# A streamed weight kernel on one core: within each half unit, all products of the high weights first, the products of the low weights last

## The chip, the cores and the metric

The kernel runs on one core of a Trainium2 chip. The metric is the device time in microseconds of one execution; lower is better. The engines are TensorE (PE, with its weight loads shown as PEld), VectorE (DVE), ScalarE (ACT), GpSimd (POOL) and SyncE (SP), which issues the stream's DMAs.

## The reference, cut to what matters

Two transformer-like blocks on 256 tokens of width 1024, all in float32. The first block mixes tokens in three ways, then has a gated feed-forward part; the second has a convolution, sparse attention, a memory attention and a layer of 16384 experts, of which each token takes a few. Nearly all of the time goes to matrix products with weights that are read once from memory:

```python
z = rmsnorm(h, norm_mix_g[l]) @ w_in[l]
...
h = h + jnp.concatenate([o_a, o_b, o_c], axis=-1) @ w_out[l]
...
u = hn @ w_up
...
return (jax.nn.silu(gate) * val) @ w_down
...
h = h + peer(rmsnorm_2(h, peer_norm_g[l]), peer_w_q[l], peer_sub_keys[l], peer_u[l], peer_v[l])
```

## The kernel before

All weights lie in one stream of units of 128 x 1024 numbers (512 KB), four units to a chunk. SP reads them in turn into four buffers `raw` (line 386). Float32 precision is had from three products of a faster type: each number is split into a high part and a low part, and the product is high x high + low x high + high x low.

A unit is split in two halves of 512 columns. `split_hi` (line 425, ScalarE) makes `w_hi` of a half and increments `s_hi1` (first half) or `s_hi` (second). `split_lo` (line 432, VectorE, or GpSimd in the woven streams and beside the selection) waits for that, makes `w_lo = raw - w_hi` and increments `s_lo1` or `s_lo`. There are two buffers each of `w_hi` and `w_lo`, so the split of a unit waits until TensorE has used the unit two before: the last product of a half increments `s_use1` or `s_use`. `halves_of_unit` (line 435) lists, for both halves, the semaphore of the low part and the one of use.

TensorE (`product3`, line 495; line 500 in the profile) takes, for each tile, the three products one behind another. Each is a weight load of 128 x 128 (PEld) and a matmul (PE). Two layouts occur. In a feature unit the weights are the loaded operand and x of 256 tokens is streamed: a half has four tiles k, 12 products of 256 columns (ps_chunk<-x_hi,w_hi in the profile). In a token unit x is loaded and 512 columns of weights are streamed: a half has one tile k and two groups t of 128 tokens, 6 products of 512 columns (ps_chunk<-w_hi,x_hi, or ps_misc<-w_hi,hid_hi). Ahead of a half TensorE waits for its low part, which comes after the high part.

The streams, in order: the mixers of the first block (to 276 us), in which `woven_products` (line 610) gives out each half in two pieces (some = 0 and 1), placed by an order written out by hand (MIXERS_ORDER, MIXERS_2_ORDER, MEMORY_ORDER) among small products of other strands; ffn_up by `multiply` (line 519), beside which VectorE does eight taps of a convolution per chunk (line 1808) between its splits; ple_proj and ffn_down by `rows_of` (line 1864); ple_gate by `multiply`; the second block's mixers and the memory, woven again; peer_q by `multiply`; 36 early rows of the experts by `u_products` (line 2704) while VectorE picks the experts (line 2603 and on): of them 32 stand ahead of some transposes (line 2687) that need VectorE's picks, and ScalarE computes in each row a gelu (line 2723), sends it off and splits a later unit; then 32 more rows between small products of the gates (line 2829); 68 units of v by `v_unit` (line 2890); and 60 pairs of a u row and a v row. In the first chunk behind a new x (`first_two`, `woven_first_two`, `woven_first_halves`, and token chunks with `by_k` or `x_made`) the products follow the making of x.

Of the kernel before, what the change touches and what calls it, by code (L numbers as in the profile page):

```python
# [215 lines left out]
def build(nc, stream, cols, rows, consts0, consts1, consts2, x, mem, positions, small_w, cmp_w1, cmp_w2, peer_keys, p_t, out):  # L216
    ctx = ExitStack()
    with ctx:
# [216 lines left out]
        halves_of_unit = ((0, s_lo1, s_use1), (1, s_lo, s_use))  # L435

# [58 lines left out]
        def product3(e, o, stationary, moving, start, stop, low_x=None):  # L495
# [6 lines left out]
            return last  # L502

# [21 lines left out]
        def multiply(name, token_major, by_k=(), between=None):  # L525
# [37 lines left out]
            def body(e, slot, n, half):  # L563
                room(e, n)
                fresh = isinstance(n, int) and n == first and by_k
                for q in range(UNITS):
# [8 lines left out]
                    for part, made, used_up in halves_of_unit:  # L575
                        e.wait_ge(made, n * UNITS + (q + 1))
                        if token_major:
                            k = 2 * q + part
                            if fresh:
                                e.wait_ge(*by_k[k][0])  # L580
                            for t in range(TT):
# [3 lines left out]
                                                by_k[k][1] if fresh else None)  # L585
# [24 lines left out]
        def woven_products(u, n, q, part, some, token_major, ps, left, x_made=None, tile_end=False):  # L610
# [3 lines left out]
            _, made, used_up = halves_of_unit[part]  # L614

            def run(e):
                e.wait_ge(made, u + 1)
                if token_major:
                    if q == 0 and part == 0 and n:
                        e.wait_ge(*left[some])  # L620
                    k = 2 * q + part
                    if x_made:
                        e.wait_ge(*x_made[k][0])
                    last = product3(e, ps[:, some * CW:some * CW + width],
                                    [x[:, k, some * P:(some + 1) * P] for x in (x_hi, x_lo)],
                                    [a[:, part * CW:part * CW + width] for a in w], k == 0, k == KD - 1,
                                    x_made[k][1] if x_made else None)
                else:
                    if q % 2 == 0 and part == 0 and some == 0 and n:
                        e.wait_ge(*left[q // 2])  # L630
# [8 lines left out]
            pe.quiet(run)  # L639

        def woven_first_two(u, ps, left, by_k, i):

# [2577 lines left out]
```

## Time and profile before

| | us |
|---|---|
| Median of 3 runs | 1593.06 |
| Lowest and highest run | 1588.82, 1595.22 |
| Span of the profiled execution | 1586.8 |
| TensorE matmuls busy | 1526.8 (96%) |
| VectorE busy | 1168.7 (74%) |
| ScalarE busy | 851.7 (54%) |
| GpSimd busy | 353.0 (22%) |

The span runs from the first to the last instruction of one profiled execution; the time of a run also holds what lies around it. Times in the rows below are microseconds from the span's start unless marked ns. Matmuls are pipelined: a matmul's own duration (0.28 us for 256 columns, 0.39 for 512) is longer than the distance between the starts of two of them, and it is that distance that tells the pace.

### The profile page before, as it was taken

What the parts mean: (1) busy time and instruction counts of PE and PEld (TensorE: products, weight loads), DVE (VectorE), ACT (ScalarE), POOL (GpSimd) and SP (SyncE); (2) the same over time, 40 slices, a digit from 0 to 9 for tenths busy, and PEclk for the clock granted to TensorE, in tenths of its full rate; (3) what the DMA queues carried; (4) which work ended last, traced back from release to release, by engine and by line L of the source; (5) the groups of instructions that cost most, each with busy time, mean ns of one, the idle gap of its engine ahead of it and who ended that gap; (6) DMA issues with size and microseconds to landing.
All of it is one profiled execution on the core that took longest, in us unless ns stands there. A gap on an engine that the chain in (4) does not pass through costs nothing.

```text
span 1586.8 us, 32061 instructions
## 1 busy us (share of the span) xinstructions
PE 1526.8 (96%) x10720; PEld 1374.3 (87%) x10720; DVE 1168.7 (74%) x2312; ACT 851.7 (54%) x1573; POOL 353.0 (22%) x265
## 2 busy tenths in 40 slices
PE   9899998999999899899999999999999999999997
PEld 7789987999887785698998999988888899999996
DVE  4788676788747577454499678889999777777776
ACT  5664445655548654565455455554444554454445
POOL 3333322011000331222067865640000000000000
PEclk9999999999999999999999999999999999999999
DMA  8332345555565720354656655467777656656564
GB/s 293 113 120 94 94 146 161 167 170 175 183 186 175 244 68 1 91 176 151 193 153 198 200 173 151 158 191 243 244 236 245 202 189 188 187 186 185 185 187 157
DMA packets 89289, 272.22 MB, mean 172 GB/s; under 512 B 9984, under 2 KB 27520, under 8 KB 88832
## 3 DMA queue, kind: packets, MB, share of 16 engines
q1 hardware_dynamic: 65520, 238.06, 47.9%
q10 hardware_dynamic: 23696, 33.17, 6.6%
q8 instruction: 48, 0.79, 0.2%
q14 instruction: 25, 0.20, 0.0%
HBM read 259.13 MB, written 12.06 MB: 171 GB/s over the span
## 4 chain that ended last, share of the span: by engine, by line
PE 77%; DVE 13%; ACT 4%; issue 2%; DMA 1%; POOL 1%; ACTq 0%; DVEq 0%; SPq 0%; POOLq 0%
PE ps_chunk L500 43%; PE ps_misc L500 22%; PE ps_misc L300 5%; PE ps_misc L2829 3%; PE ps_chunk L300 2%; DVE ffn_arena L1808 1%; DVE w_lo L432 1%; ACT w_hi L425 1%; POOL w_lo L432 1%; DVE mixers_arena L2607 1%; DVE mixers_arena L2608 1%; DVE mixers_arena L2604 1%; PE ps_chunk L507 1%; PE ps_misc L945 1%; DMA raw<-in_stream 1%
## 5 line engine op out<-in xcount | busy, mean ns | idle before, releaser
L425 ACT ACTIVATE w_hi<-raw 128x512 fp32r<-128x512 f32 (+2 forms) x898 | 547.0, 627 | 489.0 <-PE ps_chunk L500 280.8
L432 DVE TENSOR_TENSOR w_lo<-raw,w_hi 128x512 fp32r<-128x512 f32 x663 | 485.6, 748 | 256.4 <-ACT w_hi L425 246.4
L500 PE MATMUL ps_chunk<-x_hi,w_hi 128*128 128x256 f32 x1792 | 518.1, 289 | 15.3 <-POOL w_lo L432 7.6
L500 PE MATMUL ps_chunk<-x_hi,w_lo 128*128 128x256 f32 x1792 | 507.2, 283 | 0.0
L500 PE MATMUL ps_chunk<-x_lo,w_hi 128*128 128x256 f32 x1792 | 506.9, 283 | 0.0
L432 POOL TENSOR_TENSOR w_lo<-raw,w_hi 128x512 fp32r<-128x512 f32 (+2 forms) x237 | 310.1, 1323 | 517.6 <-ACT w_hi L425 453.3
L500 PEld LDWEIGHTS ps_chunk<-x_hi,w_hi 128*128 128x128 f32 x1792 | 343.2, 192 | 27.3 <-POOL w_lo L432 12.3
L500 PEld LDWEIGHTS ps_chunk<-x_hi,w_lo 128*128 128x128 f32 x1792 | 343.7, 192 | 2.7 <-issue 0.2
L500 PEld LDWEIGHTS ps_chunk<-x_lo,w_hi 128*128 128x128 f32 x1792 | 343.4, 192 | 0.0
L500 PE MATMUL ps_misc<-w_hi,hid_hi 128*128 128x512 f32 x516 | 201.7, 391 | 1.6 <-DVE hid_lo L2933 1.6
L500 PE MATMUL ps_misc<-w_hi,hid_lo 128*128 128x512 f32 x516 | 201.5, 390 | 0.0
L500 PE MATMUL ps_misc<-w_lo,hid_hi 128*128 128x512 f32 x516 | 200.7, 389 | 0.0
L300 PE MATMUL ps_misc<-mixers_arena 128*128 128x128 f32 (+9 forms) x820 | 111.0, 304 | 8.2 <-ACT mixers_arena L975 3.5
L500 PEld LDWEIGHTS ps_misc<-w_hi,hid_hi 128*128 128x128 f32 x516 | 97.1, 188 | 20.6 <-issue 1.7
L500 PEld LDWEIGHTS ps_misc<-w_lo,hid_hi 128*128 128x128 f32 x516 | 96.9, 188 | 20.7
L300 PEld LDWEIGHTS ps_misc<-mixers_arena 128*128 128x128 f32 (+3 forms) x820 | 94.7, 188 | 22.1 <-issue 8.5
L500 PEld LDWEIGHTS ps_misc<-w_hi,hid_lo 128*128 128x128 f32 x516 | 97.1, 188 | 17.7
L500 PE MATMUL ps_chunk<-w_hi,x_hi 128*128 128x512 f32 (+2 forms) x256 | 101.8, 398 | 7.2 <-POOL w_lo L432 4.6
L500 PE MATMUL ps_chunk<-w_hi,x_lo 128*128 128x512 f32 (+2 forms) x256 | 97.8, 382 | 0.0
L500 PE MATMUL ps_chunk<-w_lo,x_hi 128*128 128x512 f32 (+2 forms) x256 | 97.8, 382 | 0.0
L2929 DVE TENSOR_TENSOR xn<-row,peer_arena 128x256 f32<-128x256 f32 x128 | 80.7, 631 | 8.8 <-PE ps_misc L500 6.7
L2812 DVE TENSOR_TENSOR xn<-xn,ps_chunk 128x1024 bf16<-128x1024 bf16 x64 | 43.8, 684 | 33.0 <-PE ps_misc L2829 24.2
(411 smaller groups left out, 1667.9 us busy)
## 6 DMA issues: line engine op xcount, KB each, us to landing
raw<-in_stream SPq DMA_DIRECT2D x452, 512.0 KB, 3.6
early_rows<-row ACTq DMA_DIRECT2D x68, 128.0 KB, 1.7
row<-early_rows ACTq DMA_DIRECT2D x66, 128.0 KB, 3.3
memory_kv<-mixers_arena ACTq DMA_DIRECT2D x4, 512.0 KB, 5.0
mixers_arena<-in_cmp_w ACTq DMA_DIRECT2D x1, 2048.0 KB, 9.3
mixers_arena<-memory_kv ACTq DMA_DIRECT2D x4, 512.0 KB, 6.9
mixers_arena<-in_consts ACTq DMA_DIRECT2D x1, 1729.0 KB, 9.8
row<-in_rows ACTq DMA_DIRECT2D x3, 512.0 KB, 7.2
```

The lines of the kernel that those rows point to most:

```text
L300: return lambda e: e.matmul(out, lhsT, rhs, start=start, stop=stop, skip_group_check=True)
L425: e.activation(w_hi[q % 2][:, s], raw[q][:, s], ACT.Copy).then_inc(made, 1)
L432: e.tensor_tensor(w_lo[q % 2][:, s], raw[q][:, s], w_hi[q % 2][:, s].bitcast(F32), ALU.subtract).then_inc(made, 1)
L500: last = e.matmul(o, stationary[a], moving[b], start=start and i == 0, stop=stop and i == 2, skip_group_check=True)
L507: e.matmul(o, a[:, k * P:(k + 1) * P], x_hi[:, k, :], start=start and i == 0, stop=False, skip_group_check=True)
L945: done = pe.do(lambda e, i=i, s=s: e.transpose(ps[0:rows_out, i * P:(i + 1) * P], s, ident), *needs, *free)
L1808: e.scalar_tensor_tensor(out=o, in0=ps_chunk[slot][:, piece * T:(piece + 1) * T - lag], scalar=col[:, bass.ds(at + (2 - lag), 1)], in1=o, ...
L2604: lambda e, i: e.match_replace(out=rest[:, i, :], in_to_replace=values[:, i, 0:8], in_values=src[:, i, :], imm_value=-3e38),
L2607: lambda e, i: e.max_index(iu[:, i, 0:8], values[:, i, 0:8], src[:, i, :]),
L2812: e.tensor_tensor(twos(hot[g % 2]), iota_16.rearrange("p (n two) -> p n two", two=2).unsqueeze(1).broadcast_to(wide(2)), of_group(places_b ...
L2829: last = e.matmul(ps_misc[:, g % 2, i * P:(i + 1) * P], hot[g % 2][:, i, 1, :], gated_hot[g % 2][:, i, piece, :], start=piece == 0, stop=p ...
L2929: e.tensor_tensor(own[b], gel[slot], g, ALU.mult).then_inc(s_own, 1)
```

## The change

A list `high_of_half` names the semaphore of the high part of each half. In each half unit TensorE now waits for the high part alone, takes all products of the high weights (with x high and x low), waits for the low part, and takes the products of the low weights last. In the woven streams the two pieces of a half are cut anew: a feature half gives the high products of three tiles, then those of the fourth, the wait and the four low products; a token half gives three of its four high products, then the fourth, the wait and two low products. Left as before are the first two units behind a new x, token chunks whose x is being made, the last unit of a token stream, and in the woven projections chunk 0 and the last unit.

```diff
+        high_of_half = (s_hi1, s_hi)
...
+        def high_weights(e, o, w, k):
+
+            for x in (x_hi, x_lo):
+                e.matmul(o, w[0][:, k * P:(k + 1) * P], x[:, k, :], start=k == 0 and x is x_hi, stop=False,
+                         skip_group_check=True)
+
+        def low_weights(e, o, w, tiles):
+
+            for k in tiles:
+                last = e.matmul(o, w[1][:, k * P:(k + 1) * P], x_hi[:, k, :], start=False, stop=k == KD - 1,
+                                skip_group_check=True)
+            return last
...
                         else:
-                            for k in range(4 * part, 4 * part + 4):
-                                last = product3(e, ps_chunk[slot][:, q * T:(q + 1) * T],
-                                                [a[:, k * P:(k + 1) * P] for a in w],
-                                                [x[:, k, :] for x in (x_hi, x_lo)], k == 0, k == KD - 1)
+                            o = ps_chunk[slot][:, q * T:(q + 1) * T]
+                            tiles = range(4 * part, 4 * part + 4)
+                            e.wait_ge(high_made, n * UNITS + (q + 1))
+                            for k in tiles:
+                                high_weights(e, o, w, k)
+                            e.wait_ge(made, n * UNITS + (q + 1))
+                            last = low_weights(e, o, w, tiles)
                         last.then_inc(used_up, 1)
...
+            def by_weights(e):
+
+                k = 2 * q + part
+                outs = [ps[:, t * CW:t * CW + width] for t in range(TT)]
+                hi, lo = (a[:, part * CW:part * CW + width] for a in w)
+                if some == 0:
+                    e.wait_ge(high_made, u + 1)
+                    for t in range(TT):
+                        if q == 0 and part == 0 and n:
+                            e.wait_ge(*left[t])
+                        high_tokens(e, outs[t], k, t, hi, x_hi)
+                        if t == 0:
+                            high_tokens(e, outs[t], k, t, hi, x_lo)
+                    return
+                high_tokens(e, outs[1], k, 1, hi, x_lo)
+                e.wait_ge(made, u + 1)
+                for t in range(TT):
+                    last = low_tokens(e, outs[t], k, t, lo)
+                last.then_inc(used_up, 1)
...
         def u_products(e, b, w, u, tiles, part):
 
             _, made, used_up = halves_of_unit[part]
+            o, weights = ps_chunk[b][:, 0:T], (w_hi[w], w_lo[w])
+            e.wait_ge(high_of_half[part], u + 1)
+            for k in tiles:
+                high_weights(e, o, weights, k)
             e.wait_ge(made, u + 1)
-            for k in tiles:
-                last = product3(e, ps_chunk[b][:, 0:T], [a[w][:, k * P:(k + 1) * P] for a in (w_hi, w_lo)],
-                                [x[:, k, :] for x in (x_hi, x_lo)], k == 0, k == KD - 1)
-            if k % 4 == 3:
-                last.then_inc(used_up, 1)
+            low_weights(e, o, weights, tiles).then_inc(used_up, 1)
```

`rows_of` and `v_unit` are changed in the same way as token halves.

## Rows read from the trace of the kernel before

**Rows 1.** The page: the span; busy time by engine; chain that ended last, by engine.
```profile
span 1586.8 us, 32061 instructions
...
PE 1526.8 (96%) x10720; PEld 1374.3 (87%) x10720; DVE 1168.7 (74%) x2312; ACT 851.7 (54%) x1573; POOL 353.0 (22%) x265
...
PE 77%; DVE 13%; ACT 4%; issue 2%; DMA 1%; POOL 1%; ACTq 0%; DVEq 0%; SPq 0%; POOLq 0%
```

**Rows 2.** Waits, whole span: who <- whom: us in total, times, longest.
```profile
PEld ps_chunk L500 <- POOL w_lo L432: 18.3, 27, 2.9
...
PEld ps_chunk L500 <- DVE w_lo L432: 9.7, 15, 2.0
```

**Rows 3.** Chain that ended last in order of time: start, length, what.
```profile
750.71 40.57 PE ps_chunk L500 x336
...
1054.54 185.23 PE ps_misc L500 x816
```

**Rows 4.** Timeline of TensorE in ffn_up: start, length, instruction [idle before].
```profile
391.96 0.28 PE L500 MATMUL ps_chunk<-x_lo,w_hi 128*128 128x256 f32 x1
392.52 0.39 PE L500 MATMUL ps_chunk<-x_hi,w_hi 128*128 128x256 f32 x1 [0.28 <-DVE w_lo L432]
392.74 0.28 PE L500 MATMUL ps_chunk<-x_hi,w_lo 128*128 128x256 f32 x1
```

**Rows 5.** Waits of the weight loads, 0 to 60 us.
```profile
PEld ps_chunk L500 <- POOL w_lo L432: 1.2, 2, 0.9
```

**Rows 6.** Waits of the weight loads, 60 to 100 us; chain, 11 to 95 us.
```profile
PEld ps_chunk L500 <- DVE w_lo L432: 3.4, 2, 2.0
...
85.38 2.05 PE ps_chunk L300 x16
```

**Rows 7.** 276 to 420 us: waits; timeline of VectorE; busy time (instructions) of a chunk.
```profile
PEld ps_chunk L500 <- DVE w_lo L432: 5.5, 11, 1.1
...
391.77 2.50 DVE L432 TENSOR_TENSOR w_lo<-raw,w_hi 128x512 fp32r<-128x512 f32 x4 [0.22 <-DVE ffn_arena L1808]
...
380.47:392.52 12.05, 11.77 (x97) 11.57 (x97) 10.22 (x19) 7.19 (x14) 1.56 (x1) 1.00 0.54 174
```

**Rows 8.** 480 to 530 us: waits; timeline of ScalarE and TensorE.
```profile
PEld ps_chunk L500 <- POOL w_lo L432: 5.7, 4, 2.9
...
527.48 1.15 ACT L425 ACTIVATE w_hi<-raw 128x512 fp32r<-128x512 f32 x2 [3.03 <-DMA raw<-in_stream]
...
529.51 0.80 PE L500 MATMUL ps_chunk<-w_hi,x_hi 128*128 128x512 f32 x1 [2.68 <-POOL w_lo L432]
```

**Rows 9.** Waits of the weight loads, 660 to 800 us.
```profile
PEld ps_chunk L500 <- POOL w_lo L432: 1.0, 1, 1.0
```

**Rows 10.** The selection, 799 to 904 us: waits, then timelines of the engines.
```profile
PEld ps_chunk L500 <- POOL w_lo L432: 8.5, 18, 1.8
...
799.57 0.36 PE L500 MATMUL ps_chunk<-x_hi,w_hi 128*128 128x256 f32 x1
...
831.02 0.39 ACT L2723 ACTIVATE row<-ps_chunk 128x256 f32<-128x256 f32 x1 [1.00 <-PE ps_chunk L500]
...
832.74 2.72 POOL L432 TENSOR_TENSOR w_lo<-raw,w_hi 128x512 fp32r<-128x512 f32 x2 [0.62 <-ACT w_hi L425]
...
864.32 1.28 ACT L2635 ACT_TABLE_LOAD   x1 [0.73 <-ACT row L2723]
...
891.82 0.43 DVE L2680 CAST mixers_arena<-mixers_arena 128x512 bf16<-128x512 f32 x1
...
893.71 1.41 DVE L2680 CAST mixers_arena<-mixers_arena 128x512 bf16<-128x512 f32 x1
...
902.66 0.60 PE L2687 MATMUL ps_chunk<-ident_iota,mixers_arena 128*128 128x128 f32 x4
```

**Rows 11.** Timeline of the last row's products; chain at ple_gate's first chunk.
```profile
1576.43 0.62 PE L2907 MATMUL ps_misc<-w_lo,hid_hi 128*128 128x512 f32 x2
1576.88 0.62 PE L2907 MATMUL ps_misc<-w_hi,hid_hi 128*128 128x512 f32 x2
...
480.67 20.70 PE ps_chunk L500 x90
```

More of the change, by code:

```diff
@@ new lines, in by_tiles @@
+            def by_tiles(e):
+                o = ps[:, q * T:(q + 1) * T]
+                tiles = range(4 * part, 4 * part + 4)
+                if some == 0:
+                    e.wait_ge(high_made, u + 1)
+                    if q % 2 == 0 and part == 0 and n:
+                        e.wait_ge(*left[q // 2])
+                    for k in tiles[:3]:
+                        high_weights(e, o, w, k)
+                    return
+                high_weights(e, o, w, tiles[3])
+                e.wait_ge(made, u + 1)
+                low_weights(e, o, w, tiles).then_inc(used_up, 1)
@@ L616, in run @@
             def run(e):
                 e.wait_ge(made, u + 1)
[L618 to L630, printed above, removed]
-                    for k in range(4 * part + 2 * some, 4 * part + 2 * some + 2):
-                        last = product3(e, ps[:, q * T:(q + 1) * T],
-                                        [a[:, k * P:(k + 1) * P] for a in w],
-                                        [x[:, k, :] for x in (x_hi, x_lo)], k == 0, k == KD - 1)
+                if q == 0 and part == 0 and n:
+                    e.wait_ge(*left[some])
@@ L635, in run @@
+                k = 2 * q + part
+                if x_made:
+                    e.wait_ge(*x_made[k][0])
+                last = product3(e, ps[:, some * CW:some * CW + width],
+                                [x[:, k, some * P:(some + 1) * P] for x in (x_hi, x_lo)],
+                                [a[:, part * CW:part * CW + width] for a in w], k == 0, k == KD - 1,
+                                x_made[k][1] if x_made else None)
                 if some:
@@ L638, in run @@
                     last.then_inc(s_tile, 1)
-            pe.quiet(run)
+            pe.quiet(by_tiles if not token_major else run if x_made or by_token else by_weights)
         def woven_first_two(u, ps, left, by_k, i):
@@ L1112, in woven_projection @@
                     woven_products(u, n, q, part, some, True, ps_chunk[n % 2], ((s_ev, n - 1),) * 2,
-                                   tile_end=last and part == 1)
+                                   tile_end=last and part == 1, by_token=chunk == 0 or last)
                     if (part, some) == (0, 0):
@@ L1864, in rows_of, with times @@
             def rows_of(e, u, x, k, out, begin, end):
+                def times(t, half, x, w, start, stop):
+                    return e.matmul(out(t, half), x[:, k, t * P:(t + 1) * P], w[u % 2][:, half * CW:(half + 1) * CW],
+                                    start=start, stop=stop, skip_group_check=True)
                 for half, made, used_up in halves_of_unit:
+                    e.wait_ge(high_of_half[half], UNITS * first + u + 1)
+                    for t in range(TT):
+                        times(t, half, x[0], w_hi, begin, False)
+                        times(t, half, x[1], w_hi, False, False)
                     e.wait_ge(made, UNITS * first + u + 1)
                     for t in range(TT):
-                        last = product3(e, out(t, half), [a[:, k, t * P:(t + 1) * P] for a in x],
-                                        [w[u % 2][:, half * CW:(half + 1) * CW] for w in (w_hi, w_lo)], begin, end)
+                        last = times(t, half, x[0], w_lo, False, end)
                     last.then_inc(used_up, 1)
```

41 lines of the change are left out of this document (31 added, 10 removed).

## The prediction

> **What bounds the kernel now.** I read the page first: in the profiled execution (span 1586.8 us) TensorE is busy 96% of the time and 77% of the chain that ended last [rows 1]. So only two things can move the time: the pace of one product, and the gaps between products.
>
> The pace: in a steady stream 336 products of 256 columns take 40.57 us (121 ns each; 120 ns from start to start inside it), and 816 products of 512 columns take 185.23 us, 227.0 ns each [rows 3]. The second stretch crosses 136 half units, each with its wait for the low half, and shows no cost for them. A whole feature unit is 24 x 0.12 = 2.88 us, the eight high products of a half are 0.96 us, the four of a token half are 0.91 us.
>
> The gaps: the view of waits says that the weight loads of line 500 stood 18.3 us for a low half made by GpSimd (POOL) and 9.7 us for one made by VectorE, in 42 places [rows 2]. That is all the change can take, except that a stall also spoils the start: in the timeline the product after it starts 220 ns before the next, not 120 (392.52 to 392.74) [rows 4]. So a stall removed gives back its length and 0.10 us. At 391.96 TensorE was due again at 392.08 and began at 392.52, the low half being done at 392.46; its high half had long been made.
>
> **The change, part by part.** Removed: no product, no load, no split. Each half unit has the same products in another order and releases its buffer at its last one, as before. So no split and no DMA (SP's queue) is issued later; where TensorE comes earlier they move earlier. Added: one wait in each half unit that is changed, some 840 of about 900 (448 + 258 + 128 + 44 halves, from the counts of high products 1792/4, 516/2, 256/2, 88/2 on the page, less the first two units and the by-token ones that stay).
>
> Behind the low wait on TensorE stand the low products and everything of the other strands; before, the same stood behind it from the start of the half. VectorE is given 0.91 to 0.96 us longer in plain streams, and 0.7 us and the work of other strands between in the woven ones. The cover of the new wait is the 0.96 us of queued products; without it a wait costs the 0.10 us of a new start.
>
> The terms, by stage:
>
> 1. Start. Two waits of together 1.2 us for GpSimd's low half [rows 5]. In both the high half had been made by the time TensorE came (it must have been over 1 us earlier, since GpSimd takes 1.3 us for a low half [rows 10]). Both go: 1.2 + 2 x 0.10, less 0.1 where the high half is just made, 1.3 us. The chain runs through both on its way to VectorE. Bounds 0 and 1.4.
>
> 2. Mixers, 60 to 100 us. Two waits for VectorE's low half, 3.4 us [rows 6], and one for GpSimd's of the like, of which 0.96 us each could go. I count nothing: the chain there is VectorE's own, and TensorE's next step of it, at 85.38, waited for VectorE again [rows 6]. What is late next is the same VectorE. Bounds 0 and 2.9.
>
> 3. ffn_up and the begin of ffn_down: 11 waits, 5.5 us [rows 7], about one in each chunk of 12.05 us. In each VectorE does the eight older taps and then the low half of unit 2: 391.77 to 392.46 [rows 7], while TensorE is due at 392.08 and would need it at 392.08 + 0.96 = 393.04. So 0.58 us of slack is left, and VectorE is busy 10.22 of 12.05 us and has to fit 11.5 [rows 7]: it does. 5.5 + 11 x 0.10 = 6.6; the first of them keeps 0.3, since its high half is late too: 6.3 us. Bounds 4 and 6.6.
>
> 4. Second block, 480 to 530 us: four waits, 5.7 us [rows 8]. One lies in a chunk whose x is being made (that code is unchanged). Two lie ahead of a DMA that lands at 527.5 whatever TensorE does. At the last ScalarE waits 3.03 us for that DMA, the high half is made by 528.11, TensorE starts at 529.51 [rows 8]: 528.17 instead, 1.35 us. Bounds 0.5 and 2.8 (a part of what lies ahead of the DMA may come through too).
>
> 5. Memory, at 683: one wait of 1.0 us [rows 9], with its start 1.1; I take 1.05. Bounds 0 and 1.1.
>
> 6. Selection, 800 to 904 us: here 32 rows of 24 products run beside VectorE's top-16 work. They begin at 799.57 and end at 902.66 [rows 10]: 103.1 us, where 32 x 2.88 = 92.2. The view of waits has 18 waits, 8.5 us [rows 10]. The loop: TensorE ends a row, ScalarE's gelu of it starts 0.2 later, the DMA is issued, the next-but-one row is split (gelu at 831.02, so the row ended about 830.82), and GpSimd begins at 832.74, as soon as the first high half is there, and takes 2.72 us for both low halves (in most rows 2.55) [rows 10]. The first low half is ready at 834.09, 3.27 us after the row's end and 0.39 too late; the high one after 1.9, 1.0 early. With the change the low one is due at 2.88 + 0.96 = 3.84. The stall goes in every row, and GpSimd's 2.55 to 2.72 us fit into 2.88. One stall stays: after row 19 ScalarE loads a table at 864.32 and again after, and has the high half of row 21 only 3.5 us after the row's end [rows 10]: 0.7, then 0.4 and 0.3 for low halves, with starts 1.7 us. So the rows could end at 799.57 + 92.2 + 0.1 + 1.7 = 893.5. The transposes behind them need VectorE's last cast, done at 893.71 + 1.41 = 895.12 [rows 10]. VectorE is late next: 902.66 - 895.2 = 7.5 us. Bounds 4 and 9.
>
> 7. The rest of [rows 2]: 28.0 less 1.2, 3.4, 5.5, 5.7, 1.0 and 8.5 is 2.7 us in four places; some 1.7 of it is the third wait of term 2. With a like stall in the four selection rows behind the transposes and the starts I take 0.95; bounds 0.3 and 1.6. The gates, the early v rows and the last 330 us have no such stall: 0. There the low half is ready earlier than it need be now, and the order can only add slack.
>
> Pace of the new order, which costs or gives nothing by the nearest rows. Low products alternate between two banks of PSUM: the last row does so already, two products in 0.45 us at 1576.43 and the next at 1576.88 [rows 11], 227 each. High products of a feature half use the same weights twice: in ple_gate's first chunk that order stands today, and its stretch of 90 products takes 20.70 us with two slow starts in it [rows 11], 228 to 230 ns each, with the other order in the rest of it, about the pace of [rows 3]. Taken: 0; bounds per product -13 ns (all that lies over 256 columns at 2.4 GHz, 107 ns) and +6.
>
> Sum: 1.3 + 0 + 6.3 + 1.35 + 1.05 + 7.5 + 0.95 = 18.45 us, say 18.4, on a span of 1586.8. The median of the runs shown is 1593.06, 6.3 above that span (launch and the spread of the runs, 1588.82 to 1595.22). The gain is taken off the median: 1574.7.
>
> **The rivals.**
>
> A. VectorE's selection is held up more. GpSimd is busy 2.55 of 3.22 us per row now and would be 2.55 of 2.88. VectorE's casts of the same shape take 0.43 us at 891.82 and 1.41 at 893.71 beside GpSimd [rows 10], so something holds them for a GpSimd instruction. If the held time, which I estimate at some 20 us, grows as 0.89 to 0.79, VectorE ends 2.5 us later, at worst 4: term 6 is 3.5 to 5, the time 1577 to 1579. The Trainium skill ("SBUF — State Buffer", section "Who interferes with whom") says that VectorE instructions with two SBUF inputs or in a two-port mode and a GpSimd instruction that reads SBUF lock each other out for a whole instruction; the two durations agree with it, and by that rule the change speeds GpSimd into VectorE's way. Chance 0.15.
>
> B. What is saved early is given back at joins: terms 1, 4 and 5 vanish and term 6 halves: 6.3 + 3.7 + 0.5 (of term 7) = 10.5, 1582.6. For it: VectorE's chain at 40 to 88 us. Against: TensorE is 77% of the chain. Chance 0.10.
>
> C. More is saved: terms 2, 4 and 6 reach towards their upper bounds (1.5, 2 and 9 us) because VectorE's own waits for high halves shrink too: 18.4 + 1.5 + 0.65 + 1.5 = 22 us, 1571. Chance 0.10.
>
> D. Slower: each added wait stops TensorE's sequencer from running ahead, even when it is satisfied. At the price of a new start, 840 x 0.10 = 84 us: 1659. It decides from 18.4 / 840 = 22 ns a wait. Against it stands 227.0 ns over 136 half units [rows 3]. Chance 0.04.
>
> E. The repeated weights are cheaper at 256 columns, which no row shows: up to 13 ns on some 1790 pairs, 23 us more, 1552. Chance 0.03.
>
> Also the case that the change doesn't do what it says (stalls lie in the first two units or by-token pieces, untouched) is bounded by the waits named: it is in B.
>
> **How the numbers follow.** Forecast 0.58 at 1574.7, own range 1570 to 1580. What a measurement can tell from no change is about 0.5%, 8 us (1585.1). The range 1567 to 1584 takes in A, C and B's middle, and leaves out D, E and half of B. Faster: forecast, A, C, E and a little over half of B, less what my terms may be too large together: 0.88. Same: 0.08. Slower: 0.04.
>
> **What would show it.** In the waits of after: line 500's and the new lines' waits for low halves fall from 28.0 us to some 10, and new waits for high halves (ACT w_hi) appear only at 528 and 866. A chunk of ffn_up takes 11.5 us, not 12.05. Rows of the selection stand 2.88 us apart, and the transposes wait for VectorE. Steady streams keep 120 and 227 ns; the first product after a satisfied wait starts 120 after the one before. I am wrong if the chunks stay at 12.05, if the steady pace moves by over 1 ns, or if the saved time of the selection turns up as a wait of VectorE or GpSimd.

## The result, and the profile after

The changed kernel takes 1583.23 us (median of 8 runs, 1579.02 to 1587.94) where the kernel before, timed beside it, takes 1594.21 us (1588.82 to 1600.25). The ratio is 0.9938, 95% interval 0.9921 to 0.9956. In a second series it was 1580.81 against 1594.13 us, 0.9925 (0.9904 to 0.9945). So the change makes the kernel faster by 0.6 to 0.75%, 10 to 12 us by the ratios. The forecast was 18.4 us, and 1574.7 us. The sign holds and so does the wide range, 1567 to 1584; the forecast's own range, 1570 to 1580, doesn't. A third to nearly a half of the gain is missing.

First the page of after: the span, busy time by engine, and the chain that ended last by engine. It answers to [rows 1].

```profile
span 1583.0 us, 32051 instructions
...
PE 1526.1 (96%) x10720; PEld 1379.4 (87%) x10720; DVE 1178.0 (74%) x2312; ACT 851.2 (54%) x1573; POOL 354.2 (22%) x265
...
PE 82%; DVE 13%; ACT 2%; issue 2%; DMA 1%; POOL 0%; DVEq 0%; ACTq 0%; SPq 0%
```

The same products, and TensorE is a larger part of the chain, 82% instead of 77%. VectorE is busy 9.3 us longer with the same 2312 instructions: that is the first thing on this page that no term of the sum has in it. By stage, 3.6 us of it lie in the selection, 2.3 in ffn_up (where they cost nothing, as term 3 below shows), 2.5 ahead of 126 us and 1.0 in the second block.

Then the waits of the weight loads for a half of the weights, whole span (who, for whom: us in total, times, longest), the answer to [rows 2]. L508 and L520 are the high products of a feature half and of a token half, L514 and L524 the low ones, L501 and L529 places that keep the old order.

```profile
PEld ps_chunk L520 <- ACT w_hi L425: 2.5, 2, 1.8
...
PEld ps_chunk L508 <- ACT w_hi L425: 2.2, 3, 1.0
...
PEld ps_chunk L514 <- POOL w_lo L432: 2.0, 5, 0.6
...
PEld ps_chunk L524 <- POOL w_lo L432: 1.1, 3, 0.6
PEld ps_chunk L514 <- DVE w_lo L432: 1.1, 1, 1.1
PEld ps_chunk L501 <- POOL w_lo L432: 1.1, 1, 1.1
...
PEld ps_chunk L524 <- DVE w_lo L432: 0.9, 2, 0.7
...
PEld ps_chunk L529 <- POOL w_lo L432: 0.5, 1, 0.5
...
PEld ps_chunk L501 <- DVE w_lo L432: 0.4, 1, 0.4
```

The low halves' waits add up to 7.1 us, where they were 28.0, and waits for the high half are 4.7 us in five places. So the change does what it says. What was taken away is 16.2 us of waits. To see where it went I took the start of the same VectorE instruction in every profile (the 2312 of them stand in one order in all these kernels) and subtracted those of the first profile of before. The table has, by stage of the kernel before, how much longer or shorter each stage is, in us, and in brackets how long the granted clock stood at 1.2 GHz, not 2.4, inside it (the last 5 to 9 us of every profile, which are at 1.2 GHz too, are left out). The second profile of each kernel is from the experiments e8 and e12 below.

| stage, us of before | before, 2nd | after | after, 2nd |
|---|---|---|---|
| 0 to 40, start | +1.32 (3.4) | -0.06 (0) | -0.29 (3.4) |
| 40 to 126, mixers | +2.99 (10.2; 6.8 in the first of before) | +7.46 (20.4) | +1.53 (6.8) |
| 126 to 283, mixers | +1.06 (3.4) | +1.44 (3.4) | -0.08 (0) |
| 283 to 428, ffn_up, ffn_down | -0.02 | -6.31 | -6.33 |
| 428 to 523 | -0.06 | +0.02 | +0.02 |
| 523 to 660, second block | +3.72 (23.8; 17.0 in the first) | -2.17 (13.6) | -2.66 (13.6) |
| 660 to 700, memory | +0.04 | -0.85 | -0.93 |
| 700 to 800 | -0.02 | -0.42 | -0.42 |
| 800 to 925, selection | +0.04 | -2.78 (3.4) | -2.82 (3.4) |
| 925 to the end | +0.18 | -0.11 | -0.16 |
| sum | +9.2 | -3.8 | -12.1 |

Two things are to be seen. The rows for ffn_up, memory and the selection agree to 0.1 us in both profiles of a kernel: they are the program's. The start, the mixers and the second block don't, and differ in one kernel by up to 6 us, by and large with the brackets: most of that goes with the clock. And the profile from which I worked, 1586.8 us, was the fastest of the 8 runs of before shown here.

The stage where the forecast fails is the selection, -2.8 where the terms said -7.5. The timelines of after, TensorE at the transposes and the last operations of VectorE ahead of them, answer to [rows 10]:

```profile
898.00 1.02 PE L2759 MATMUL ps_chunk<-ident_iota,mixers_arena 128*128 128x128 f32 x4 [5.16 <-DVE mixers_arena L2752]
```

```profile
894.97 1.48 DVE L2754 TENSOR_TENSOR mixers_arena<-mixers_arena 128x256 f32<-128x256 f32 x1
896.49 1.37 DVE L2752 CAST mixers_arena<-mixers_arena 128x512 bf16<-128x512 f32 x1
```

TensorE ends its 32 rows at 892.8, as forecast (893.5, less the 0.9 us by which after is ahead at 800 us, the sum of the table down to there), and then stands idle for 5.16 us. VectorE's last cast ends at 897.86. In before it ended at 895.12 [rows 10]; less the 0.9 us it would be 894.2, so VectorE's work in this stage has grown by some 3.6 us. Groups of VectorE's instructions between 800 and 905 us (busy us, mean ns), first before, then after:

```profile
L2664 DVE TENSOR_REDUCE mixers_arena<-mixers_arena 128x256 f32<-128x4096 f32 x2 | 8.8, 4420 | 0.1
...
L2629 DVE TENSOR_TENSOR mixers_arena<-mixers_arena 128x256 f32<-128x256 f32 (+1 forms) x5 | 4.9, 972 | 0.2
...
L2680 DVE CAST mixers_arena<-mixers_arena 128x512 bf16<-128x512 f32 x3 | 3.3, 1106 | 0.1
```

```profile
L2701 DVE TENSOR_TENSOR mixers_arena<-mixers_arena 128x256 f32<-128x256 f32 (+1 forms) x5 | 6.7, 1348 | 0.2
...
L2752 DVE CAST mixers_arena<-mixers_arena 128x512 bf16<-128x512 f32 x3 | 4.1, 1380 | 0.1
...
L2749 DVE CAST mixers_arena<-mixers_arena 128x512 bf16<-128x512 f32 x2 | 1.8, 964 | 0.0
```

The five sums take 1.8 us more and the three casts 0.8; the other two casts took 0.8 us before (L2677) and take 1.8. That is 3.6 us. Beside this stand GpSimd's low halves from 835 to 895 us, before and after: 37 in 60 us became 42, and its idle time for ScalarE's high halves fell by half.

```profile
L432 POOL TENSOR_TENSOR w_lo<-raw,w_hi 128x512 fp32r<-128x512 f32 x37 | 48.9, 1340 | 12.0 <-ACT w_hi L425 11.9
```

```profile
L432 POOL TENSOR_TENSOR w_lo<-raw,w_hi 128x512 fp32r<-128x512 f32 x42 | 56.2, 1362 | 6.1 <-ACT w_hi L425 5.8
```

In the mixers the first profile of after shows two long waits of TensorE (40 to 110 us) and, in the windows of 20 us, the clock (third figure from the end of a line: the mean granted clock as a share of 2.4 GHz; 0.74 is half of the time at 1.2):

```profile
PE ps_misc L300 <- DVE mixers_arena L1560: 2.8, 1, 2.8
PE ps_misc L1010 <- DVE mixers_arena L1588: 2.6, 1, 2.6
```

```profile
60.00:80.00 20.00, 17.90 (x121) 16.59 (x120) 13.85 (x15) 10.39 (x18) 5.26 (x5) 0.87 0.38 116
80.00:100.00 20.00, 17.40 (x119) 16.82 (x119) 13.80 (x16) 13.24 (x17) 5.04 (x4) 0.74 0.25 82
```

In the first profile of before the first of these waits was 0.3 us long and the second 0.2, and from 60 to 100 us the clock stood at 2.4 GHz throughout.

### The profile page after: what moved, and what is told of

The parts are those of the page before. It is cut to its first block, busy times and chain, and to the rows that moved or that the text cites. A ratio compares the mean times of both kernels' runs of the same rounds, so it can differ in the third digit from the quotient of the medians.

```text
span 1583.0 us, 32051 instructions
## 1 busy us (share of the span) xinstructions
PE 1526.1 (96%) x10720; PEld 1379.4 (87%) x10720; DVE 1178.0 (74%) x2312; ACT 851.2 (54%) x1573; POOL 354.2 (22%) x265
## 4 chain that ended last, share of the span: by engine, by line
PE 82%; DVE 13%; ACT 2%; issue 2%; DMA 1%; POOL 0%; DVEq 0%; ACTq 0%; SPq 0%
PE ps_chunk L508 22%; PE ps_misc L2966 22%; PE ps_chunk L514 11%; PE ps_misc L300 6%; PE ps_chunk L1931 4%; PE ps_chunk L501 3%; PE ps_chunk L520 3%; PE ps_misc L2901 3%; PE ps_chunk L300 2%; PE ps_chunk L524 2%; PE ps_chunk L529 1%; PE ps_misc L1010 1%; DVE mixers_arena L2680 1%; DVE mixers_arena L2679 1%; DVE mixers_arena L2676 1%
## 5 line engine op out<-in xcount | busy, mean ns | idle before, releaser
L508 PE MATMUL ps_chunk<-x_hi,w_hi 128*128 128x256 f32 x1792 | 459.0, 288 | 2.0 <-ACT w_hi L425 1.6
L508 PE MATMUL ps_chunk<-x_lo,w_hi 128*128 128x256 f32 x1792 | 452.3, 285 | 0.0
L508 PEld LDWEIGHTS ps_chunk<-x_hi,w_hi 128*128 128x128 f32 x1792 | 345.8, 193 | 6.2 <-ACT w_hi L425 2.2
L508 PEld LDWEIGHTS ps_chunk<-x_lo,w_hi 128*128 128x128 f32 x1792 | 346.6, 193 | 2.9 <-issue 0.5
L514 PE MATMUL ps_chunk<-x_hi,w_lo 128*128 128x256 f32 x1792 | 290.0, 285 | 1.9 <-DVE w_lo L432 0.9
L514 PEld LDWEIGHTS ps_chunk<-x_hi,w_lo 128*128 128x128 f32 x1792 | 248.4, 193 | 3.2 <-POOL w_lo L432 2.0
L2966 PE MATMUL ps_misc<-w_hi,hid_hi 128*128 128x512 f32 x508 | 198.3, 390 | 1.6 <-issue 1.6
L2966 PE MATMUL ps_misc<-w_lo,hid_hi 128*128 128x512 f32 x508 | 156.9, 390 | 0.0
L520 PE MATMUL ps_chunk<-w_hi,x_hi 128*128 128x512 f32 (+2 forms) x160 | 60.9, 385 | 2.3 <-ACT w_hi L425 2.1
L2795 ACT ACTIVATE row<-ps_chunk 128x256 f32<-128x256 f32 x68 | 26.1, 384 | 64.0 <-PE ps_chunk L514 63.9
L520 PE MATMUL ps_chunk<-w_hi,x_lo 128*128 128x512 f32 (+2 forms) x160 | 59.9, 378 | 0.0
## 6 DMA issues: line engine op xcount, KB each, us to landing
mixers_arena<-in_cmp_w ACTq DMA_DIRECT2D x1, 2048.0 KB, 10.2
```

What stands on the lines that cost most here:

```text
L508: e.matmul(o, w[0][:, k * P:(k + 1) * P], x[:, k, :], start=k == 0 and x is x_hi, stop=False, skip_group_check=True)
L514: last = e.matmul(o, w[1][:, k * P:(k + 1) * P], x_hi[:, k, :], start=False, stop=k == KD - 1, skip_group_check=True)
L520: return e.matmul(o, x[:, k, t * P:(t + 1) * P], w, start=k == 0 and x is x_hi, stop=False, skip_group_check=True)
L2966: return e.matmul(ps_misc[:, 2 * t + half, :], x[:, b, t * P:(t + 1) * P], weights[w][:, half * CW:(half + 1) * CW], start=start, stop=Fal ...
```

## The experiments

The theory after this reading had two parts. In the selection GpSimd, no longer held back by TensorE, splits more densely and lengthens VectorE's small operations. In the first mixers the woven order saves small waits which come back as two long ones, and behind these the clock falls. The rivals: the missing gain is only spread between runs, since the profile of before was its fastest; or VectorE's lengthening has another cause.

### One half of the change at a time

e1 has the new order in the plain streams alone. Its woven pieces use the body of before, here called as_before:

```
-            pe.quiet(by_tiles if not token_major else run if x_made or by_token else by_weights)
+            pe.quiet(as_before if True else by_tiles if not token_major else run if x_made or by_token else by_weights)
```

> The new order in the plain streams alone (multiply, the rows of ffn_down, the rows of the experts' u and v); every woven product stands as in the kernel before. Theory (the woven products of the first mixers save TensorE small waits, which come back there as two long ones, 2.8 us for VectorE's L1560 and 2.6 us for L1588, and behind each the granted clock falls to 1.2 GHz, so that this kernel's stage from 40 to 270 us costs 9.3 us more than before's): that stage comes out as in the profile of before, only the second block's 1.8 us are given up, so the time is about 1583 - 9.3 + 2 = 1576 us, ratio 0.989, and TensorE's wait for L1560 is under 0.5 us. Rival (the profile of before was merely its luckiest run, and a typical one loses as much in the mixers; the woven order costs nothing): 1583 + 2 = 1585 us, ratio 0.994, with two falls of the clock between 55 and 95 us all the same.

Measured: 1585.16 us against 1594.27, ratio 0.9933 (0.9909 to 0.9958), which is the rival's number. Its profile has falls of the clock at 48 and 72 us (3.4 us each), and TensorE's wait for L1560 is 2.0 us, where the theory had under 0.5. The selection behaves as in after, with a wait of 5.2 us ahead of the transposes; the fall behind it is 6.8 us long here and the stage only 1.6 us shorter than in before.

e2 is the other half: multiply, rows_of, u_products and v_unit stand as before, the woven order is new. Of u_products, against after:

```
-            o, weights = ps_chunk[b][:, 0:T], (w_hi[w], w_lo[w])
-            e.wait_ge(high_of_half[part], u + 1)
+            e.wait_ge(made, u + 1)
             for k in tiles:
-                high_weights(e, o, weights, k)
-            e.wait_ge(made, u + 1)
-            low_weights(e, o, weights, tiles).then_inc(used_up, 1)
+                last = product3(e, ps_chunk[b][:, 0:T], [a[w][:, k * P:(k + 1) * P] for a in (w_hi, w_lo)],
+                                [x[:, k, :] for x in (x_hi, x_lo)], k == 0, k == KD - 1)
+            if k % 4 == 3:
+                last.then_inc(used_up, 1)
```

> The new order in the woven products alone; the plain streams stand as before. Theory (long joins and the clock behind them in the first mixers): the gain of about 2 us in the second block against a loss of up to 9 us in the first mixers, so slower than before: 1594 + 9 - 2 = 1601 us if before's profile is typical there, and at least 1595 us. Rival (the woven order costs nothing, before's profile was its luckiest run): 1594 - 2 = 1592 us.

Measured: 1594.88 us against 1594.27, ratio 0.9996 (0.9972 to 1.0020). Neither 1601 nor clearly 1592. Its profile gains 0.9 us in memory and has no fall at 529, but has TensorE's 2.6 us wait for the same VectorE instruction as after and a fall of 10.2 us at 78. So almost the whole gain is the plain streams', and the woven order gives nothing in sum that these intervals show.

e3 keeps the new order in the woven pieces of the second block and memory and takes it back in the first.

```
-            pe.quiet(by_tiles if not token_major else run if x_made or by_token else by_weights)
+            pe.quiet(as_before if n < STREAM["ffn_up"][0] else by_tiles if not token_major else run if x_made or by_token else by_weights)
```

> The changed kernel with the products woven into the first block (all streams ahead of ffn_up) back in the order of before; everything else of the change stays. Theory (first mixers lose 7 to 9 us to long joins and the clock): 1583 - 8 = 1575 us, ratio 0.988, falls of the clock ahead of 270 us as in before's profile (one, at 47.8 us). Rival (run-to-run spread): 1583 us as the changed kernel, and falls of the clock at about 58 and 82 us here too.

Measured: 1580.17 us, ratio 0.9909 (0.9885 to 0.9933), against 0.9938 and 0.9925 for the changed kernel in its two series. The direction would be the theory's, but the intervals overlap, and the size (8 us) is not there: it had been read from one pair of profiles, one lucky and one unlucky. Nor are the falls where the theory had them: e3's profile has none at 47.8 us and two at 71 and 263 us.

### Was it the profile of before?

e8 is the kernel before and e12 the changed one, each for a second profile.

> The kernel before, unchanged, for a second profile of it. The runs shown of it span 1588.8 to 1600.3 us, and the profile that the prediction was made from was of the fastest, with one fall of the granted clock ahead of 500 us. Theory (falls of the clock differ from run to run, and that profile had fewer than most): a span of 1590 us or more and at least one fall between 60 and 500 us. Rival (the program sets them all): the same seven falls at the same times.

> The changed kernel, unchanged, for a second profile and for the runs of this call. Theory (the falls behind the two long joins of the first mixers come in each run, but with 3.4 to 10.2 us each): 1583 us within 2 us, TensorE's waits for L1560 and L1588 again 2 to 3 us, and falls of the clock behind at least one of them; VectorE's five sums take 6.7 us again. Rival (the first profile was an accident in its waits too): waits under 1 us.

Measured: e8 1597.83 us, span 1596.0; e12 1580.81 us (0.9925), its profile 1574.7 us. The waits of TensorE from 40 to 110 us, in e8 and in e12:

```profile
PE ps_misc L300 <- DVE mixers_arena L1495: 2.0, 1, 2.0
...
PE ps_misc L945 <- DVE mixers_arena L1523: 0.2, 1, 0.2
```

```profile
PE ps_misc L1010 <- DVE mixers_arena L1588: 2.6, 1, 2.6
PE ps_misc L300 <- DVE mixers_arena L1560: 1.9, 1, 1.9
```

L1495 of before is L1560 of after, L1523 is L1588. The first long wait is in both kernels in a usual run; 0.3 us in the first profile of before was the exception, since the clock had been at 1.2 GHz for 6.8 us shortly ahead of it and TensorE came late anyway. e2, with a like fall at 47 us, has 0.2 us there. The second, 2.6 us, stands in each of the six profiles with the new woven order and no fill, and is 0.2 or less without it: that is the program's, and it is saved time given back. Falls of the clock differ from run to run in both: e8 has them at 60, 74 and 265 us where the first profile of before has none. Not all of them do: the four at 584, 604, 638 and 652 us of before stand in all four profiles of the two kernels at the same VectorE instructions, within 0.4 us. So each of the two views under e8 is right for a part of the falls. I had compared a best run with a middling one: by that pair the kernel gains 3.8 us and loses 8.9 between 40 and 283 us.

Over all profiles, the stage from 40 to 283 us is longer than in the first profile of before by 0, 4.1, 3.0, 2.4 and 3.2 us in the five with the old woven order there (before, e8, e1, e3, e9), mean 2.5, and by 8.9, 1.4, 3.4, 2.6, 3.9 and 5.2 in the six with the new one (after, e12, e5, e6, e7, e2), mean 4.3. So the new order may lose some 1.7 us there; the two sets overlap, and this number is not shown.

### Is it the clock or the wait?

e4 puts products that nobody reads on TensorE ahead of the three joins:

```
-            done = pe.do(mm(ps, head_ones, X2), v, *free)
+            pe.wait(*free)
+            for _ in range(22):
+                pe.quiet(mm(ps[:, 0:P], ident, ident))
+            done = pe.do(mm(ps, head_ones, X2), v)
```

and the like ahead of the transposes behind L1588 (22) and of the selection's (40).

> The changed kernel with products of the identity, which nobody reads, put on TensorE ahead of three joins: 22 (about 2.5 us) ahead of the product that waits for L1560, 22 ahead of the transposes that wait for L1588, and 40 (about 4.6 us) ahead of the transposes of the selection. The joins come no earlier, but TensorE doesn't idle ahead of them. Theory that the clock's fall behind the idle stretch is the larger part of the loss: the falls at 58.4 (6.8 us), 82.3 (10.2 us) and 898.1 us (3.4 us) go, half of those 20.4 us comes back less what the earlier falls of before's profile show to be there anyway, so 7 to 10 us less: 1574 to 1576 us. Theory that the waits themselves are the loss: 1583 us, within 1 us.

Measured: 1586.87 us, ratio 0.9950 (0.9928 to 0.9971), if anything slower than the changed kernel. But I had mis-sized the fill: the timeline has 22 of them as 44 records, 5.07 us against a wait of 2.8.

```profile
56.76 5.07 PE L300 MATMUL ps_misc<-ident_iota 128*128 128x128 f32 x44
```

No fall of the clock was left between 12 and 260 us, so the first half of the theory held even here, while 84 x 0.227 = 19.1 us of fill stood against 10.6 us of waits. e10 has 11, 11 and 20 of them.

> The kernel of the filled joins with half as many products of the identity: 11, 11 and 20. One of them took 0.227 us in e4_filled_joins, twice what had been assumed, so that 84 of them, 19.1 us, stood against 10.6 us of waits. Here they are 2.5, 2.5 and 4.5 us, inside the waits of 2.8, 2.6 and 5.2 us. Theory that the clock behind the long joins is what the first mixers and the selection lose: 1583 - 5 (first mixers) - 1.7 (selection) = 1576 us, and no fall of the clock at 58, 82 and 898 us. Theory that the fall comes whatever TensorE does there, or that the waits are all of the loss: 1583 us.

Measured: 1577.99 us (1574.24 to 1584.34), ratio 0.9919 (0.9897 to 0.9940). Its timeline at the first join and at the selection's, and then the windows from 60 to 100 us:

```profile
56.53 2.62 PE L300 MATMUL ps_misc<-ident_iota 128*128 128x128 f32 x22
...
883.73 4.62 PE L300 MATMUL ps_misc<-ident_iota 128*128 128x128 f32 x40
...
888.97 0.66 PE L2768 MATMUL ps_chunk<-ident_iota,mixers_arena 128*128 128x128 f32 x4 [0.62 <-DVE mixers_arena L2759]
```

```profile
60.00:80.00 20.00, 17.92 (x147) 17.31 (x146) 15.58 (x19) 13.37 (x21) 7.12 (x5) 1.00 0.33 107
80.00:100.00 20.00, 19.44 (x154) 17.71 (x154) 15.54 (x17) 16.60 (x23) 5.44 (x4) 1.00 0.41 132
```

The joins come no earlier, TensorE has more to do, and yet the stage from 40 to 283 us is the shortest of all the kernels with the new order (+0.6; +1.6 in e11 below, which has the same fill there, inside the 1.4 to 8.9 of those without) and the selection gains 4.4 us instead of 2.8. In the profiles of e4, e10 and e11 no fall begins between 54 and 260 us; of the eleven without a fill ten have one. So in these profiles it is TensorE's idling that brings the fall; in those with the old order of the first mixers (e8, e1, e3, e9) one comes at 71 to 74 us, behind a wait of 1.8 us for a low half, which the change removes. In the selection 3.4 us at 1.2 GHz cost 1.6 us (4.4 - 2.8), and 6.8 us in e1 cost 2.8 (4.4 - 1.6), where the join itself came at the same time, within 0.1 us. By the profile of e10 the fill gives 4.3 - 0.6 + 1.6 = 5.3 us, and with the mean of e10 and e11 in the mixers 4.8. The times don't show it: by the ratios e10 is 3 us under the first series of after and 1 us under the second, and the intervals overlap.

### The selection

e6 sets only the products of the experts' rows of u back to the order of before (the diff shown under e2, alone), e7 keeps the new order and makes GpSimd's part small (it leaves out most of the low halves of these rows, so its results aren't the layer's):

```
-                with e.Fori(1, EARLY // 4) as c:
+                with e.Fori(1, EARLY_SELECT // 4 - 1) as c:
+                    for q in range(UNITS):
+                        split_lo(e, q, c + chunk_early, width=16)
+                with e.Fori(EARLY_SELECT // 4 - 1, EARLY // 4) as c:
                     for q in range(UNITS):
                         split_lo(e, q, c + chunk_early)
```

> The changed kernel with the products of the experts' rows of u (the early rows of the selection, those between the groups, and the later ones) in the order of before; the rest of the change stays. Theory (the selection gives back 2.7 us, because GpSimd, no longer held by TensorE, splits more densely beside VectorE and lengthens its small operations): VectorE's five sums (L2629 of before, L2701 of after) take 4.9 us again instead of 6.7, its three casts 3.3 instead of 4.1, TensorE's wait at the transposes is under 1 us, and the whole is 1583 + 3 = 1586 us. Rival (VectorE's operations are slower for a reason outside this stage, such as its place in time or the woven products): 6.7 and 4.1 us here too, and more than 1586 us.

> The changed kernel in which GpSimd computes the low halves of the weights for the early rows 4 to 31 over 16 columns of each half unit instead of 512, so that those rows lack most of their low products' data; every wait and every product stays. GpSimd is then nearly idle beside VectorE's selection. Theory (VectorE is held by GpSimd's splitting): the five sums take 4.9 us or less, the three casts 3.3 or less, VectorE's last cast ends 3 us or more earlier than in the changed kernel (897.9 us there, taken with respect to the begin of its selection). Rival (the port is not the cause, only the time at which the rows go): 6.7 and 4.1 us as in the changed kernel.

Measured: e6 1582.79 us, 0.9939 (0.9922 to 0.9956); e7 1579.67 us in one run. The groups of VectorE in the selection, first e6, then e7:

```profile
L2701 DVE TENSOR_TENSOR mixers_arena<-mixers_arena 128x256 f32<-128x256 f32 (+1 forms) x5 | 4.9, 972 | 0.2
...
L2752 DVE CAST mixers_arena<-mixers_arena 128x512 bf16<-128x512 f32 x3 | 3.3, 1097 | 0.1
```

```profile
L2736 DVE TENSOR_REDUCE mixers_arena<-mixers_arena 128x256 f32<-128x4096 f32 x2 | 8.8, 4420 | 0.1
...
L2701 DVE TENSOR_TENSOR mixers_arena<-mixers_arena 128x256 f32<-128x256 f32 (+1 forms) x5 | 1.9, 372 | 0.2
...
L2752 DVE CAST mixers_arena<-mixers_arena 128x512 bf16<-128x512 f32 x3 | 1.3, 426 | 0.1
```

With the old order of the rows VectorE is back at the figures of before. With GpSimd nearly idle a sum takes 372 ns, where it takes 972 beside the old order and 1348 beside the new. This is the cause of VectorE's late end, shown from both sides. It also repeats: counted from VectorE's instruction at 800 us, the last cast ends 3.6 or 3.7 us later than in the first profile of before in each of the nine profiles with the new order of the rows and GpSimd's full splits (after, e12, e1, e3, e4, e5, e9, e10, e11), within 0.03 us of it in e8, e2 and e6, and 16.8 us earlier in e7. The reductions, with one input each, take 4420 ns in before, in e6 and in e7. The Trainium skill ("SBUF — State Buffer", section "Who interferes with whom") says just this: VectorE instructions with two SBUF inputs or in a two-port mode and GpSimd's reads shut each other out, and a reduction is never held. The traces agree, by 372 against 972 and 1348 ns, and by 4420 in each.

The stage from 800 to 925 us is 0.0 in e6 and -10.2 us in e7, against -2.8 in after. In e7 no product waits for VectorE any more and TensorE begins the transposes 9.6 us earlier than in before: its rows alone would have allowed that. So the first part of term 6 was right. In time e6 was expected at 1586 us and isn't there: by the ratios it is the same as the first series of after and 2.2 us slower than the second, within the intervals; the stage in the profiles is the better measure.

e5 leaves VectorE's work alone but uses TensorE's wait: two of the four rows behind the transposes go ahead of them.

```
                 if last:
-                    four(EARLY_SELECT // 4 - 1)
+                    four(EARLY_SELECT // 4 - 1, range(2, UNITS))
                     return
                 four(0)
                 with e.Fori(1, EARLY_SELECT // 4 - 1) as c:
                     four(c)
+                four(EARLY_SELECT // 4 - 1, range(2))
```

> The changed kernel with two of the four rows that TensorE computes behind the selection's transposes put ahead of them: 34 rows ahead and 2 behind, where it was 32 and 4. No work is added or left out. Two rows are 5.8 us of products, TensorE's wait for VectorE's last cast was 5.2 us. Theory (in the selection TensorE comes early and waits, and the granted clock is at 1.2 GHz for 3.4 us behind the wait): the wait goes, 5.2 - 0.6 and up to 1.7 us are saved, 1577 to 1579 us. Rival (the wait only moves: the group products or ScalarE's rows take it up): 1583 us within 1 us, with a wait of 4 us or more ahead of the first group products.

Measured: 1579.08 us (1569.68 to 1580.44), ratio 0.9905 (0.9880 to 0.9930). The transposes and the first products of a group behind them:

```profile
892.36 0.60 PE L2759 MATMUL ps_chunk<-ident_iota,mixers_arena 128*128 128x128 f32 x4
...
899.20 0.84 PE L2902 MATMUL ps_misc<-xn 128*128 128x128 bf16 x12
```

No idle time is shown at either, and the stage is 9.7 us shorter than before, 6.9 us more than in after: the 5.2 us of wait and 1.7 us of the fall with it. By the ratios e5 is 3 to 5 us under after, and the intervals overlap; the stage is -9.7 us again in e9 and in e11.

### Both mends

e9 has the edits of e3 and e5 together, e11 the fill of e10 in the mixers (11 and 11) and the moved rows of e5.

> The changed kernel with both mends that the trace suggests: the products woven into the first block in the order of before (as e3) and two rows of the selection moved ahead of its transposes (as e5). Theory (two places, independent of one another): 1583 - 3 - 4.5 = 1575.5 us, ratio 0.988 or less. Rival (the gains of the two are run-to-run spread or overlap): 1579 us or more.

> The changed kernel with its new order everywhere, 11 products of the identity ahead of each of the two joins of the first mixers (as e10) and the two rows moved ahead of the transposes (as e5). Theory (what the woven order loses in the first mixers is the clock behind the joins, so filling them is worth as much as undoing the order there): 1583 - 3.5 - 4.5 = 1575 us, within 1.5 us of e9_both_mends. Rival (the fill costs TensorE time that the clock doesn't give back): 1579 us or more, behind e9_both_mends by over 2 us.

Measured: e9 1574.11 us (1571.28 to 1580.48), ratio 0.9890 (0.9867 to 0.9913); e11 1577.04 us (1569.17 to 1579.25), 0.9884 (0.9858 to 0.9909). By the ratios they are the same, and both are faster than the kernel before by 1.1%, 18 us; by the medians they are 2.9 us apart, more than the 1.5 that e11's theory allowed. So whether the fill is worth as much as the old order there stays open. What the order of the first mixers or their fill adds to e5 is within the intervals: 0.9905, 0.9890, 0.9884. The moved rows are what is sure, by their stage in three profiles.

## Why the prediction was right or wrong

The terms against their stages, with sizes from the profiles:

1. Start, 1.3 us: it is won (0.99 us at 27 us in the first profile of after) and 0.93 of it is given back by 40 us. There ScalarE, in the timeline of after, waits for the weights' DMA, which it didn't have to before:

```profile
32.14 1.15 ACT L425 ACTIVATE w_hi<-raw 128x512 fp32r<-128x512 f32 x2 [1.76 <-DMA raw<-in_stream]
```

   The two profiles of after leave 0.06 and 0.29 us against the first profile of before. Such a giving back was in rival B. But it isn't in every profile: e2, whose clock doesn't fall there either, keeps 0.89 us at 40 us, and after's second profile is 1.6 us under before's second, both with a fall at 9 us. So the size of this term stays open, between 0.1 and 1.6 us.
2. Mixers, 0 with bounds 0 to 2.9: the profiles rather point at a loss, 1.7 us, which is not shown. I had said what is late next, VectorE, and stopped there, without the price of TensorE standing there in one piece (the wait of 2.6 us for L1588) and the clock behind it, so that the bounds had no room for a loss.
3. ffn_up and the begin of ffn_down, 6.3: 6.31 and 6.33, and between 6.1 and 6.5 in every kernel with it. There isn't a wait for a weight left from 284 to 428 us. A half unit takes 1.44 us and so a chunk of eight 11.5, as forecast. Chain of after, early in ffn_up:

```profile
301.54 0.96 PE ps_chunk L508 x8
302.50 0.48 PE ps_chunk L514 x4
302.98 0.96 PE ps_chunk L508 x8
```

4. Second block, 1.35: perhaps too small. The stage from 523 to 660 us is 0, +3.7 and +3.8 us in the three profiles with the old woven order and -0.5 in the mean of the eleven with the new (-3.1 to +6.8), so some 3 us by the means, which such a spread doesn't show. In the first profile of before the clock went to 1.2 GHz at 529.1, within the very wait of 2.68 us in [rows 8]; in after that wait is 1.57 us, for the high half, and the fall isn't there. That fall is in all three profiles with the old order, and still in four of the eleven with the new (e4, e6, e7, e11: -0.4 to +6.8 us); the seven without it have -1.2 to -3.1. I had priced the wait and not the fall.
5. Memory, 1.05: 0.85 and 0.93.
6. Selection, 7.5: 2.8, of which some 0.6 is the four rows behind the transposes that term 7 had. This is the step that failed. Its first part held: the rows run at 2.88 us, and TensorE is done with them at 892.8. The sentence "VectorE is late next: 902.66 - 895.2" took VectorE's end from the profile of before as if the change could not move it. It moved by 3.6 us, for GpSimd, and TensorE's 5.2 us of idling brought a fall of the clock, 1.6 us more. Rival A had the mechanism, the rows and the rule, and with 2.5 to 4 us the right size for VectorE's end, though not the fall behind it; the mistake was to give it 0.15, when all that speaks for it was in [rows 10]: the change makes GpSimd denser by construction, and two casts of one shape took 0.43 and 1.41 us.
7. The rest, 0.95: 0.42 from 700 to 800, 0.17 in the later rows and the 0.6 just named, 1.2.

Pace: no price and no gift. The chain has 816 products of 512 columns in 185.24 us, as in [rows 3], and 12 products of 256 columns in 1.44 us, 120 ns each, by the chain lines under 3. Rival D (22 ns a wait) and rival E are refuted by these:

```profile
419.33 61.85 PE ps_chunk L1931 x264
...
1050.90 185.24 PE ps_misc L2966 x816
```

The first is ffn_down, 234 ns a product; the same 264 products took 62.10 us in before's chain.

With these sizes the sum is 0.2 - 1.7 + 6.3 + 3.0 + 0.9 + 2.2 + 1.2 = 12.1 us; by the ratios it is 10 and 12. ffn_up, the memory, the selection and the rest agree between profiles and make 10.6 us (6.3 + 0.9 + 2.2 + 1.2); the start, the mixers and the second block are within the spread of the clock, so that their part of the sum is an estimate. What is missing from 18.4 is the selection (5.3), the mixers (1.7, the least certain) and the start (1.1); the second block gives 1.65 of it back and the rest 0.25. Rival B's number, 1582.6 us, is the nearest to the measured 1583.23, but by luck: it has terms 4 and 5 vanish, which they don't, half of term 6 lost, where it was over two thirds, and its mechanism, time given back at a join, is not what took most of it.

One more step was weak: the gain was taken off the median, but its terms were read from a run 4.2 us faster than that (1588.82 against 1593.06). It happened to do no harm to the sum, since the terms that count stand in both profiles of before; it did harm to the reading of after.

## What to carry to other kernels

When a wait is taken away, the work that it held back on a third engine gets denser; look up whose instructions that engine lengthens before taking an end time over from the old profile. Where the saved time collects in one wait ahead of a join, put existing work of the same engine ahead of it (two rows, 7 us here) rather than accept the wait. Take two profiles of the kernel before, and trust the stages on which they agree.

## What the runs showed of the hardware that I had not expected

A fall of the granted clock to 1.2 GHz came in or just behind idle stretches of TensorE of only 1.8 to 3.2 us, not in each run, and one of 3.4 us cost 1.6 us in the selection. Spread between runs of one kernel goes with it: in the first series with e1 the 18 runs of the kernel before go from 1589.5 us at a mean granted clock of 0.990 to 1599.8 us at 0.982. And idling can be worse than useless work: 2.6 us of products that nobody reads, put into a wait of 2.8 us, made the kernel no slower (0.9919 against 0.9938 and 0.9925) and kept the clock up.
